# Taking a local-attention row maximum one operation of the inversion later, in the queue of the vector engine

## The reference, cut to what matters

```python
# delta rule, for each chunk of 64
t_inv = triangular_solve(eye + m, eye)            # inverse of a unit lower triangle
u, w = t_inv @ (v*beta), t_inv @ (k_beta*exp(g))
v_new = u - w @ state
o = (q*exp(g)) @ state + a_intra @ v_new
state = state*exp(g_last) + k_dec.T @ v_new
# window attention, for each block of 128 queries and each head
mx = maximum(max(scores, -1), sink)
p = exp(scores - mx)
out = (p / (sum(p) + exp(sink - mx))) @ v
```

## Time and profile before

| | us |
|---|---|
| median of 3 runs | 2415.31 (2412.03 to 2415.86) |
| profiled execution | 2408.52 |
| its span, first to last instruction | 2406.7 |
| PE busy in the span | 2172.6 (90%) |
| DVE busy | 1161.2 (48%) |
| ACT busy | 730.5 (30%) |
| POOL busy | 374.5 (16%) |

### The profile page before, as it was taken

The page is one execution under the profiler, slowest core; times in us unless marked ns, Lnnn a source line. Parts: engine busy times, 40 slices in busy tenths (PEclk is TensorE's granted clock), DMA queues, the critical chain, the costliest instruction groups (busy, mean ns, idle before and its releaser), DMA issues. The chain is left out here.

```text
span 2406.7 us, 33809 instructions
## 1 busy us (share of the span) xinstructions
PE 2172.6 (90%) x14386; PEld 1682.5 (70%) x14414; DVE 1161.2 (48%) x1691; ACT 730.5 (30%) x1263; POOL 374.5 (16%) x305
## 2 busy tenths in 40 slices
PE   3999996888987899999948788899999999999998
PEld 2888884567766677777725354677878878878877
DVE  4575333666665764222167466546442443342443
ACT  3222313233332343111131466444221321221321
POOL 3000002222223651000032221252000000000000
PEclk9999997799898899999968899999999999999999
DMA  3212332000001745454200400322112112111112
GB/s 125 99 44 73 93 97 83 1 2 2 2 2 46 245 131 175 131 166 149 85 17 2 189 1 1 114 79 62 44 40 57 44 35 61 45 42 55 44 37 86
DMA packets 185209, 168.98 MB, mean 70 GB/s; under 512 B 13448, under 2 KB 163804, under 8 KB 184932
## 3 DMA queue, kind: packets, MB, share of 16 engines
q1 hardware_dynamic: 179006, 146.77, 19.5%
q0 software_dynamic: 5360, 19.92, 2.1%
q10 hardware_dynamic: 694, 0.13, 0.0%
HBM read 138.49 MB, written 28.31 MB: 69 GB/s over the span
## 5 line engine op out<-in xcount | busy, mean ns | idle before, releaser
L246 PE MATMUL mix_acc<-mix_hi,w_hi 128*128 128x512 f32 x1040 | 410.1, 394 | 8.6 <-DVE w_lo L234 8.6
L248 PE MATMUL mix_acc<-mix_hi,w_lo 128*128 128x512 f32 x1040 | 408.7, 393 | 0.0
L247 PE MATMUL mix_acc<-m_lo,w_hi 128*128 128x512 f32 x1040 | 408.6, 393 | 0.0
L229 ACT ACTIVATE w_hi<-w_stage 128x1024 fp32r<-128x1024 f32 x160 | 169.0, 1056 | 614.0 <-PE mix_acc L248 259.0
L234 DVE TENSOR_TENSOR w_lo<-w_stage,w_hi 128x1024 fp32r<-128x1024 f32 x160 | 199.6, 1248 | 229.3 <-ACT w_hi L229 229.3
L2750 DVE SCALAR_TENSOR_TENSOR hidden<-mix_acc,hidden_conv,hidden 128x1023 f32<-128x1023 f32 x88 | 112.9, 1282 | 263.5 <-ACT hidden L2709 261.9
L246 PEld LDWEIGHTS mix_acc<-mix_hi,w_hi 128*128 128x128 f32 x1040 | 195.3, 188 | 56.8 <-DVE w_lo L234 12.4
L248 PEld LDWEIGHTS mix_acc<-mix_hi,w_lo 128*128 128x128 f32 x1040 | 195.3, 188 | 45.1
L247 PEld LDWEIGHTS mix_acc<-m_lo,w_hi 128*128 128x128 f32 x1040 | 195.4, 188 | 44.3
L246 PE MATMUL acc<-h_hi,w_hi 128*128 128x512 f32 x432 | 170.8, 395 | 4.8 <-DVE h_lo L631 4.8
L247 PE MATMUL acc<-h_lo,w_hi 128*128 128x512 f32 x432 | 169.1, 391 | 0.0
(11 more groups left out here) (311 smaller groups left out, 3545.9 us busy)
## 6 DMA issues: line engine op xcount, KB each, us to landing
w_stage<-in_w_in SPq DMA_DIRECT2D x48, 512.0 KB, 5.4
w_ada<-in_w_ada SPq DMA_DIRECT2D x48, 512.0 KB, 4.8
w_stage<-in_w_up SPq DMA_DIRECT2D x44, 512.0 KB, 3.7
w_stage<-in_w_out SPq DMA_DIRECT2D x32, 512.0 KB, 4.1
spill<-y_tok POOLq DMA_DIRECT2D x24, 512.0 KB, 4.5
m_resid<-resid_spill SPq DMA_DIRECT2D x2, 4096.0 KB, 14.5
conv_in<-spill SPq DMA_DIRECT2D x3, 2048.0 KB, 12.3
w_stage<-in_w_down SPq DMA_DIRECT2D x16, 384.0 KB, 3.4
```

Source lines behind the costliest of these rows:

```text
L229: nc.scalar.activation(w_hi[:, slot], w_stage[:, slot], ACT.Copy).then_inc(w_hi_ready, 1)
L246: nc.tensor.matmul(acc[:, h, :], w_hi[:, slot, k, :], hi[:, k, tok], start=k == 0, stop=False)
L247: nc.tensor.matmul(acc[:, h, :], w_hi[:, slot, k, :], lo[:, k, tok], start=False, stop=False)
L248: mm = nc.tensor.matmul(acc[:, h, :], w_lo[:, slot, k, :], hi[:, k, tok], start=False, stop=k == kts - 1)
```

## The change

DVE's part of a score step, `maxima(u)` (L1392 and L1394), is taken out of `in_gap` and put into a function `maxima_of` of its own, which is called one inversion operation of DVE further down its queue. In a gap (lv, 0) it was ahead of `inv_add(s, lv)` and is now behind it and its transpose. In a gap (lv, 1) it was ahead of `corner_mask(s, lv + 1)` and is now behind it; in the gap (5, 1) it was ahead of `scores_of(s + 1)` and is now behind `scores_of(s + 1)` and the three operations of `first_inverse(s + 1)`. The queues of PE, ACT, POOL and SP are as before, and so are all semaphores, tiles and instructions.

```diff
                     kind, u = window_step(gap)
+                    if kind == "turn1":
+                        copy_turned(u)
+
+                def maxima_of(s, lv, f):
+                    gap = gap_of(s, lv, f)
+                    if gap is None:
+                        return
+                    kind, u = window_step(gap)
                     if kind == "score":
                         maxima(u)
-                    elif kind == "turn1":
-                        copy_turned(u)
...
                     if s < NCH:
                         first_inverse(s)
+                    if s:
+                        maxima_of(s - 1, LEVELS - 1, 1)
                     in_gap(s, 0, 0)
                     if s:
                         subtract_state(s - 1)
+                    maxima_of(s, 0, 0)
                     for lv in range(LEVELS):
                         if s < NCH and lv:
                             corner_mask(s, lv)
+                        if lv:
+                            maxima_of(s, lv - 1, 1)
                         if s and lv == 5:
                             advance(s - 1, 1)
                         if lv:
                             in_gap(s, lv, 0)
                         if s < NCH and lv:
                             inv_add(s, lv)
+                        if lv:
+                            maxima_of(s, lv, 0)
```

## The result

The change made the kernel slower: 2478.73 us median (2461.42 to 2486.54, 6 runs) against 2413.67 for the kernel before in the same comparison, a ratio of 1.0273 (95% interval 1.0246 to 1.0301), or some 66 us. The direction was forecast; the time lies outside the range of 2434 to 2468.

The account below looks back on a forecast made before the run. Round trips between engines, not one engine's throughput, were taken to set the stage. Gap delays less the gain sum to 27.7 us, giving 2443 us; 5 us for the clock makes 2448 us, range 2434 to 2468.

Parts of the forecast that it names:

- The mechanism and its sign: Score stage: a later maximum delays ACT's exponentials and copy, so PE waits at `turn1`; slower, at 93%.
- The delay in (5,1): Six scores behind `first_inverse`: `turn1` about 2.8 us later, loss taken as 2.4 us each, 14.4 us in all.
- The delays in (1,1), (4,1), (0,1) and (2,1): Scores behind `corner_mask`: losses of 3.5, 4.8, 5.6 and 1.2 us through later exponentials and copy.
- + 0.8: Gap (4,1): the reduction starts 0.8 us later and all of it reaches `gram`, 6 x 0.8 = 4.8 us.
- the 1.6 us that it was to add: Gap (0,1): L1394 meets POOL's product and ends later, making the loss 5.6 us instead of 4.0.
- The gain in (3,0): Seven scores: `inv_add` need not wait behind the maximum and starts 0.46 us earlier in three instances; 1.8 us won.
- the clock's term: PE's granted clock falls behind waits for ACT's copy; six new waits at the present waits' mean cost 5 us.
- the single case of 8.0 us: Step from 632 us: PE's clock falls to half behind a wait for ACT's copy, a loss of 8.0 us.
- the clock becomes the main cost: Rival, 12%: PE stays at half clock for a whole step, up to six times 8.0 us: 2468 to 2491 us.
- The inversion's chain: Rival, 4%: the inversion sets the time and attention has room; only gains stand, -7.4 us, 2408 us, faster.
- neither condition set for the sum: Sum wrong if `turn1` in (5,1) starts under 2 us later, or PE's wait for L1241 stays under 12 us.
- The expected count of 24 to 30 waits: PE's waits for ACT's L1241 at 24 to 30 places instead of 12, 30 us or more instead of 8.6.

Follow-up runs that it names:

- experiment 5: The changed kernel with ACT's copy of unit u's first transposes put ahead of the exponentials of unit u+1: 2412.43 us, ratio 1.0000.
- experiment 2: Only the scores of gaps (0,1), (1,1), (4,1) and (2,1) late, the others as in the kernel before: 2441.83 us, ratio 1.0144.
- experiments 8 and 11: The kernel before with twelve idle matmuls in the turn1 of gap (1,1), 2391.54 us; the same with only the (3,0) scores late, 2389.65 us.
- experiment 6: The kernel before with ACT's copy put ahead of the next unit's exponentials, no score late: 2408.15 us, ratio 0.9978.
- experiment 10: Scores of (0,1), (1,1), (4,1), (2,1) late, with idle matmuls in turn1 of (1,1) (24) and (3,0) (8): 2408.71 us, ratio 0.9995.

## Why the prediction was right and wrong

- **The mechanism and its sign** hold. PE waits for ACT's copy behind the late maximum, and experiment 5 undoes the loss, but for some 4 us, by nothing but the order of copy and exponentials on ACT.
- **The delay in (5,1)**, 2.4 us each and 14.4 in all, measured 14 to 16. PE's wait of 2.76 us answers to the 2.8 worked out.
- **The delays in (1,1), (4,1), (0,1) and (2,1)**, 15.1 us in all, measured 12 to 13 by the stretches, 10 by the medians. In (4,1) five waits grew from 0.68 to 1.47 and the sixth from 0.20 to 0.99, as + 0.8 asked for. In (1,1) no wait of PE for L1241 appears in the changed kernel's 18: all six scores fall into stretches at half clock, begun behind (5,1). In experiment 2, where (5,1) is not late, the six waits are there, 3.8 us in all, close to the 3.5. In (2,1) the wait grew by 1.2, as said. In (0,1) the rows of before were misread. L1394 does not take 0.16 us in five of six there: it takes 0.16 in one, 0.85 in one, and 0.33 or 0.34 in the other four, which already run beside POOL's `v_rest` products. One of them, at the score after the one at 544 us:

```profile
590.11 0.33 DVE L1394 SCALAR_TENSOR_TENSOR max_neg<-row_max,sink_neg 128x2 f32<-128x2 f32 x1
```

In the changed kernel it takes 0.16 us in two, 0.20 in one, and 0.40, 0.66 and 0.75 in the other three: 2.3 us in all, against 2.4 before. So POOL's block added nothing; the 1.6 us that it was to add (5.6 instead of 4.0) were not there.

- **The gain in (3,0)**, 1.8 us, measured 0.9 to 1.1 by the stretches and 1.9 between the medians of experiments 8 and 11, which the spread of the runs does not separate.
- **The step that failed is the clock's term**: "At the mean of the dozen present waits (8.0 and three times 0.7, over 12) six new ones cost 5 us. I add 5". It measured about 46. It took the new waits for more of the old kind. But behind the old ones, of 0.2 to 0.9 us, the clock fell in four of twelve cases, and behind the new ones of 2 to 3.6 us in twelve of twelve. The place in the step counts too: in (0,1) it fell four times of six already before, in (4,1) never, and there the waits of up to 1.47 us brought two falls in six. And the term counted six new waits, although the (0,1) waits, 0.89 plus 1.1, would by its own sum be 2 us long too. Spread over the twelve long waits the 46 us are 3.9 us each: half of the single case of 8.0 us that the prediction had read, and several times the mean of 0.8 that it used. The rival "the clock becomes the main cost" had this mechanism and, with 2468 to 2491 us, the right time, at 12%. That its time is right is partly luck: it has up to six waits at 8.0 us each, where twelve at 3.9 were found.
- **The inversion's chain** as the opposite rival: with the copy out of the way (experiment 5) it should have come out; it gave no gain against the kernel before and a loss of 4 us against experiment 6. The earlier masks do take waits of PE away, but those for DVE's copy and ahead of `gram` grow by more.
- **What would show it wrong**: neither condition set for the sum was met. The expected count of 24 to 30 waits was 18; their total, 30 us or more, was 39.9. There was more time at half clock, 116 us more, which was to bear out the last term; it shows that the term was there, at nine times its size.

## What to carry to other kernels

Where a small operation moves in one engine's queue, ask what stands behind it on the next engine: here a copy that another engine waited for was behind two exponentials, and that was nearly the whole delay. In a stage of small matmuls and round trips like this one, price every new wait of PE twice, once as itself and once as the time at half clock that may follow it; behind waits of about 2 us and more it followed every time. If PE has to wait in such a stage, a few idle matmuls in the wait are worth a try: twelve of them, six times, made the kernel before 0.9% faster with nothing else changed but the wait on `s_pair`.

## What the runs showed of the hardware

- In the stretch of the scores, over the profiles of all fourteen kernels, PE has 31 waits of 1.85 to 3.59 us. For each of them a time at half clock (1.2 GHz) begins within the wait or at most 2.2 us after its end. Of the 36 waits of 1.38 to 1.47 us this holds for 23.
- In this stage a microsecond at 1.2 GHz instead of 2.4 costs 0.38 to 0.43 us, over five pairs of kernels. `corner_sum` (16 matmuls 64x32) takes 1.07 instead of 0.66 us.
- The twelve idle matmuls in one gap of every second step took the time at half clock from 47.9 to 10.2 us; the same twelve at another gap, where PE does not wait, left it at 51.2.
- L1394, a tiny operation with two SBUF inputs, takes 0.16 us, and up to 0.99 us (in experiment 10, from 593.83 us) while POOL works on products in SBUF; it ended there 0.02 us behind the POOL operation that ran beside it (593.76 to 594.80).
